# Small loads, turned conv tails, a split weight pair and token products reordered in a one-core decoder step

## The reference

```python
h = rmsnorm(x, norm_mix)
(m_q, m_k, m_v, m_i, m_f, m_o, g_qkv, g_a, g_b, g_out, x_q,
 gate_a, gate_b, gate_c) = split(h @ w_in)
h_a, C1, n1, m1 = mlstm_chunked(...)            # matrix memory, 4 heads of 128
conv_in = concatenate([conv0, g_qkv], axis=1)   # causal conv of width 4
conv1 = conv_in[:, S:]                          # the conv tails: an output
h_b, S1 = gated_delta_chunked(silu(conv(conv_in)), ...)
h_c = memory_attention(x_q, mem_k, mem_v)       # prompt: rmsnorm(mem, mem_norm) @ w_mem_kv; samples: caches
mixed = (sigmoid(gate_a) * (h_a @ w_br_mlstm) + sigmoid(gate_b) * (h_b @ w_br_gdn)
         + sigmoid(gate_c) * (h_c @ w_br_xattn))
x = x + mixed @ w_out
x = x + hier_moe(rmsnorm(x, norm_ffn), ...)     # top-1 of 4 groups, top-2 of 4 experts in it
y = rmsnorm(x, final_norm)
```

## Time and profile before

| | |
|---|---|
| median of 3 runs | 776.87 us (774.41 to 777.2) |
| profiled execution, its own time | 773.82 us |
| its span, first to last instruction | 771.7 us |
| PE busy | 716.7 us |
| DVE busy | 274.6 us |
| ACT busy | 164.5 us |
| bytes moved by DMA | 187.25 MB |
| mean granted TensorE clock | 0.98 |

### The profile page before, as it was taken

How to read it: one execution, slowest core, us unless ns; L and a number is a source line. 1 busy time by engine, 2 the same in 40 slices (tenths; PEclk the granted TensorE clock), 3 DMA queues, 4 the chain that set the end, 5 groups by cost and what they waited for, 6 DMA issues and landing times.

```text
span 771.7 us, 10609 instructions
## 1 busy us (share of the span) xinstructions
PE 716.7 (93%) x4393; PEld 422.0 (55%) x4393; DVE 274.6 (36%) x732; ACT 164.5 (21%) x377; POOL 62.3 (8%) x93
## 2 busy tenths in 40 slices
PE   6999999999989999999999999999999877878784
PEld 3544457877656777777777775543333323323331
DVE  1242013566763761464154352250232101100245
ACT  3221212222455411321131211231010000000014
POOL 3010200010330100000010020020000000001110
PEclk9999999999999999999999999999999989999998
DMA  9983700661399502023325487677999999999991
GB/s 271 343 284 109 192 27 1 236 252 72 96 393 371 187 6 106 1 84 138 109 73 214 138 278 315 243 314 259 391 424 427 407 429 430 411 425 398 431 358 64
DMA packets 49471, 187.25 MB, mean 243 GB/s; under 512 B 5240, under 2 KB 5485, under 8 KB 45322
## 3 DMA queue, kind: packets, MB, share of 16 engines
q1 hardware_dynamic: 40032, 155.52, 52.1%
q0 software_dynamic: 9280, 30.96, 12.1%
q10 hardware_dynamic: 106, 0.03, 0.0%
HBM read 174.43 MB, written 16.83 MB: 248 GB/s over the span
## 4 chain that ended last, share of the span: by engine, by line
PE 74%; DMA 15%; DVE 5%; ACT 2%; issue 2%; SPq 1%; POOL 1%; ACTq 0%; DVEq 0%
PE PS L664 13%; PE PS L1011 12%; DMA arena<-in_w_exp_down 9%; PE PS L1428 8%; PE PS L1023 6%; PE PS L1458 6%; PE PS L753 5%; DMA ring<-in_w_exp_down 3%; PE PS L675 2%; PE PS L780 2%; DMA out_C_s<-ring 2%; PE PS L650 2%; PE PS L1310 2%; PE PS L739 1%; SPq L1533 1%
## 5 line engine op out<-in xcount | busy, mean ns | idle before, releaser
L1428 PE MATMUL PS<-ring,arena 128*64 128x512 f32 x416 | 98.5, 629 | 13.7 <-issue 13.7
L1011 PE MATMUL PS<-hT,ring 128*128 128x288 f32 x384 | 102.2, 414 | 0.0
L1762 ACT ACTIVATE arena<-PS 128x512 f32<-128x512 f32 (+7 forms) x128 | 51.0, 422 | 183.5 <-PE PS L664 51.3
L1011 PEld LDWEIGHTS PS<-hT,ring 128*128 128x128 f32 x384 | 70.1, 190 | 19.6 <-issue 1.5
L1428 PEld LDWEIGHTS PS<-ring,arena 128*64 128x64 f32 x416 | 34.6, 144 | 73.0 <-issue 73.0
L664 PE MATMUL PS<-ring,hT 128*128 128x512 f32 x160 | 70.3, 596 | 0.0
L1762 ACT ACTIVATE brT<-PS 128x256 f32<-128x256 f32 (+4 forms) x37 | 15.6, 424 | 200.1 <-PE PS L1428 152.6
L1023 PE MATMUL PS<-brT,ring 128*128 128x288 f32 x192 | 50.5, 412 | 0.3 <-DVE arena L2557 0.3
L664 PEld LDWEIGHTS PS<-ring,hT 128*128 128x128 f32 x160 | 29.9, 190 | 37.3 <-issue 37.3
L753 PE MATMUL PS<-hT,ring 128*128 128x288 f32 x192 | 49.3, 410 | 0.9 <-DVE small L2325 0.9
L2968 DVE SCALAR_TENSOR_TENSOR brT<-brT,PS 128x256 f32<-128x256 f32 x16 | 6.7, 421 | 113.5 <-ACT brT L1762 113.5
(11 more groups left out here) (393 smaller groups left out, 866.9 us busy)
## 6 DMA issues: line engine op xcount, KB each, us to landing
ring<-in_w_in SPq DMA_DIRECT2D x15, 2048.0 KB, 10.3
ring<-in_w_exp_gate SPq DMA_DIRECT2D x13, 2048.0 KB, 23.9
ring<-in_w_exp_up SPq DMA_DIRECT2D x13, 2048.0 KB, 26.3
ring<-in_w_exp_down SPq DMA_DIRECT2D x8, 2048.0 KB, 26.0
arena<-in_w_exp_down SPq DMA_DIRECT2D x6, 2048.0 KB, 29.8
arena<-in_w_exp_gate SPq DMA_DIRECT2D x3, 2048.0 KB, 17.6
arena<-in_w_exp_up SPq DMA_DIRECT2D x3, 2048.0 KB, 22.4
moe_in<-in_table SPq DMA_DIRECT2D x2, 2048.0 KB, 23.8
```

Source lines behind the costliest of these rows:

```text
L1011: ins = pe.matmul(PS[:, b, 0:T], w[:, 512 * k + 128 * (c % 4):512 * k + 128 * (c % 4) + 128], hT[:, k, :], start=(k == 0), stop=(k == KD - 1))
L1428: ins = pe.matmul(o[64 * hf:64 * hf + 64, :], hg[:, k, 64 * e:64 * e + 64], w[:, :, 512 * k + 256 * hf:512 * k + 256 * hf + 256], start=(k ...
L1762: return act.activation(o, i, f, **kw)
```

## The change

- The memory norm gets a tile of its own (`memrow`), loaded first on ACT's queue, turned into bank 7 and copied by DVE ahead of the first memory tile; the other five vectors are turned after the second memory tile.
- On ACT, `keys_out(4)` stands ahead of `silu(0)`, whose tanh waits for the output of C_s.
- The twelve transposes of the conv tails go from the end of the attention to behind the router's last logits; ACT's copies go behind the three normalised rows, ACT issues the two output DMAs itself, and DVE waits for these before its first write of selected slots (`hg` shares the memory). Old waits for them are gone. The fillers go from 4 and 3 to 3 and 1.
- Pair 4 (the down matrices of experts 0 and 1 of group 0) is loaded as four DMAs of 1 MB: two when PE has read half of pair 0's matrices, two when it has read all.
- In the last group `to_tokens(0, 0)` and `to_samples(0)` stand ahead of the third gate/up instead of behind it, with other banks, and DVE's additions move accordingly.
- The four loads of S signal one semaphore instead of four.

```diff
@@ tensor
-        pe.wait_ge(sg("vrow_in"), 16 * 6)
-        o = use("vec", 6)
-        pe.transpose(o[:, 0:NV], vrow, ident[0:NV, 0:NV]).then_inc(full[6], 1)
+        pe.wait_ge(sg("mem_norm_in"), 16)
+        o = use("memvec", 7)
+        pe.transpose(o[:, 0:KD], memrow, ident[0:KD, 0:KD]).then_inc(full[7], 1)
         pe.wait_ge(sg("xin4"), 16)
         turn_rows(4, (2, 3))
+        pe.wait_ge(sg("vrow_in"), 16 * 5)
+        o = use("vec", 6)
+        pe.transpose(o[:, 0:NV - KD], vrow, ident[0:NV - KD, 0:NV - KD]).then_inc(full[6], 1)
...
         read_memory(1)
-        pe.wait_ge(sg("tailT"), 1)
-        for g in range(3):
-            b = (0, 5, 6)[g]
...
         logits(1).then_inc(full[1], 1)
-        keep_busy(4)
+        pe.wait_ge(sg("tailT"), 1)
+        for g in range(3):
+            b = (0, 5, 4)[g]
+            o = use(("tail", g), b)
+            for c in range(4):
+                ins = pe.transpose(o[0:HIST * (NB + 1), 128 * c:128 * c + 128], tailT[:, 4 * g + c, :], ident)
+            ins.then_inc(full[b], 1)
+        keep_busy(3)
...
-        keep_busy(3)
+        keep_busy(1)
...
             down(0, p, g)
+            to_tokens(0, 0, p)
+            to_samples(0, p)
             gate_up(2, p, g)
-            to_samples(0, p)
-            to_tokens(0, 0, p)
             to_tokens(0, 1, p)
...
+                if (g, e, k) == (0, 0, KD // 2 - 1) and isinstance(p, int):
+                    ins.then_inc(sg("half_read"), 1)
@@ sync
+            if first and q == NPAIR:
+                sp.wait_ge(sg("half_read"), 1)
+                for ex in range(2):
+                    ...
+                    sp.dma_start(dst[:, 0:2, :], src[:, 0:2, :]).then_inc(sg("d_first"), 16)
+                sp.wait_ge(*last_reader(0, p))
+                for ex in range(2):
+                    ...
+                    sp.dma_start(dst[:, 2:4, :], src[:, 2:4, :]).then_inc(ring_full[gslot("d", ex, 0)], 16)
+                return
@@ gpsimd
-        pool.wait_ge(*taken(("tail", 2)))
-        pool.dma_start(out["conv_p"][0, 0], tails[0:HIST, :]).then_inc(sg("tail_out"), 16)
-        pool.dma_start(out["conv_s"][0].rearrange("b s c -> (b s) c"), tails[HIST:, :]).then_inc(sg("tail_out"), 16)
@@ scalar
+        act.dma_start(memrow, a["mem_norm"][0].rearrange("(r c) -> r c", c=128)).then_inc(sg("mem_norm_in"), 16)
...
+        keys_out(4)
         silu(0)
-        keys_out(4)
...
-        act.wait_ge(sg("Cp_out"), 16)
-        for g in range(3):
-            copy_out(("tail", g), tails[:, 512 * g:512 * g + 512], bank_of(("tail", g))[0:HIST * (NB + 1), :])
...
+        for g in range(3):
+            copy_out(("tail", g), tails[:, 512 * g:512 * g + 512], bank_of(("tail", g))[0:HIST * (NB + 1), :])
+        act.wait_ge(*taken(("tail", 2)))
+        act.dma_start(out["conv_p"][0, 0], tails[0:HIST, :]).then_inc(sg("tail_out"), 16)
+        act.dma_start(out["conv_s"][0].rearrange("b s c -> (b s) c"), tails[HIST:, :]).then_inc(sg("tail_out"), 16)
         act.wait_ge(sg("lge"), 1)
@@ vector
             if g == 0:
+                if isinstance(p, int):
+                    dve.wait_ge(sg("tail_out"), 32)
                 slots_out(0, p, 0)
...
                     add_rows(0, p, step)
+                    add_tokens(0, 0, 0, p)
+                    add_tokens(0, 0, 1, p)
+                    add_samples(0, p)
                 if (e, g) == (2, G - 1):
-                    add_samples(0, p)
-                    for nn in range(2):
-                        for t in range(2):
-                            add_tokens(0, nn, t, p)
+                    add_tokens(0, 1, 0, p)
+                    add_tokens(0, 1, 1, p)
```

More of the change, by code:

```diff
@@ L160, in build @@
     tailT = tiny(128, NCT, HIST * (NB + 1))
-    V_MIX, V_MEM, V_ML, V_GD, V_FFN = 0, KD, 2 * KD, 2 * KD + H, 2 * KD + H + 1
+    V_MIX, V_ML, V_GD, V_FFN = 0, KD, KD + H, KD + H + 1
     V_N0 = V_FFN + KD
+    V_MEM = V_N0 + NB * H
     cwT = tiny(128, NCT, NB * HIST + CW)
@@ L250, in build @@
     wg, p = place(p, 128, KD, 16)
-    vrow, p = place(p, NV, 128)
+    vrow, p = place(p, NV - KD, 128)
+    memrow, p = place(p, KD, 128)
     crow, p = place(p, NB * HIST + CW, CCH)
@@ L290, in build @@
     qwm, _ = place(M0 + NB * DA, 128, H, NB, NS)
-    tails, _ = place(M0 + 4 * W, HIST * (NB + 1), CCH)
+    tails, _ = place(M0, HIST * (NB + 1), CCH)
     mixed, p = place(B0, 128, KD, T)
@@ L1188, in _ @@
                 hp = [slice(NS * h, NS * h + NS) for h in range(H)]
-                for h in range(H):
-                    pe.wait_ge(sg(f"Ss_in{h}"), 16)
+                pe.wait_ge(sg("Ss_in"), 16 * H)
                 pe.wait_ge(sg("qdm"), 1)
@@ L1451, in down @@
                         pe.wait_ge(*gready("d", 2 * pr_ + x, p, g))
+                    if (g, pr_) == (0, 0) and isinstance(p, int):
+                        pe.wait_ge(sg("d_first"), 32)
                 pe.wait_ge(*gtaken("dn", 2 * pr_ + nn, p, g))
@@ L1506, in load_pair @@
             s_ = PAIR_SLOTS[q % NPAIR]
+            if first and q == NPAIR:
+                sp.wait_ge(sg("half_read"), 1)
+                for ex in range(2):
+                    src = a["w_exp_down"][0, ex].rearrange("(c p) n -> p c n", p=128)
+                    dst = gunit("d", ex, 0).rearrange("p (c n) -> p c n", c=4)
+                    sp.dma_start(dst[:, 0:2, :], src[:, 0:2, :]).then_inc(sg("d_first"), 16)
+                sp.wait_ge(*last_reader(0, p))
+                for ex in range(2):
+                    src = a["w_exp_down"][0, ex].rearrange("(c p) n -> p c n", p=128)
+                    dst = gunit("d", ex, 0).rearrange("p (c n) -> p c n", c=4)
+                    sp.dma_start(dst[:, 2:4, :], src[:, 2:4, :]).then_inc(ring_full[gslot("d", ex, 0)], 16)
+                return
             if q >= NPAIR:
@@ L1762, in run @@
             return act.activation(o, i, f, **kw)
+        act.dma_start(memrow, a["mem_norm"][0].rearrange("(r c) -> r c", c=128)).then_inc(sg("mem_norm_in"), 16)
         r = 0
-        for x, n in ((a["norm_mix"][0], KD), (a["mem_norm"][0], KD), (a["mlstm_norm"][0], H),
-                     (a["gdn_norm"][0], 1), (a["norm_ffn"][0], KD)):
+        for x, n in ((a["norm_mix"][0], KD), (a["mlstm_norm"][0], H), (a["gdn_norm"][0], 1), (a["norm_ffn"][0], KD)):
             act.dma_start(vrow[r:r + n, :], x.rearrange("(r c) -> r c", c=128)).then_inc(sg("vrow_in"), 16)
@@ L2041, in _ @@
             part_at(t, "X0")
-            if t == 0:
-                act.wait_ge(sg("tail_out"), 32)
-            else:
+            if t:
                 act.wait_ge(*filled(("hbT", t - 1)))
@@ L2217, in mark @@
             dve.memset(scrap[:, marks[0]:marks[0] + 1], 0.0).then_inc(sem_, n)
-        dve.wait_ge(*filled("vec"))
-        cp(vecT, bank_of("vec")[:, 0:NV]).then_inc(freed("vec"), 1)
-        dve.wait_ge(*taken("vec"))
+        dve.wait_ge(*filled("memvec"))
+        cp(vecT[:, V_MEM:V_MEM + KD], bank_of("memvec")[:, 0:KD]).then_inc(freed("memvec"), 1)
+        dve.wait_ge(*taken("memvec"))
         for j in (3, 4, 0, 1, 2):
@@ L2224, in _ @@
             if j == 0:
+                dve.wait_ge(*filled("vec"))
+                cp(vecT[:, 0:NV - KD], bank_of("vec")[:, 0:NV - KD]).then_inc(freed("vec"), 1)
+                dve.wait_ge(*taken("vec"))
                 for i, (_, m) in enumerate(TILES):
```

5 lines of the change are left out of this document (2 added, 3 removed).

## The result

The changed kernel takes 770.57 us (median of 7 runs, 767.09 to 772.47) against 777.11 for the kernel before beside it (7 runs, 774.29 to 779.03): ratio 0.9927, 95% interval 0.9908 to 0.9945, so 4.3 to 7.1 us faster. A second series (experiment 8) gave 771.27 (11 runs) against 774.43 (16 runs), ratio 0.994, interval 0.9919 to 0.996: 3.1 to 6.3 us. The forecast was 770.9 and 6.0 us.

What follows compares the result with a forecast made beforehand. The prediction took a PE chain to bound the kernel until the weight stream fills at 539.81, then bytes. Its terms, 4.5 us ahead and 1.5 behind, make 6.0 off the median 776.87: 770.9 us, range 766.5 to 775.5.

Steps and rivals of the forecast that it cites:

- start of kvK: At the kernel's start, the norm's own load lets the first projection matmuls begin near 10.2 instead of 11.57: 1.4 us.
- keys' copy: In the key turns, copying keys before the tanh shortens PE's 1.86 us wait: 1.2 us, ends 0.6 and 1.6.
- tails out of the middle: After attention, the transposes only cover a wait (0), but ACT's lighter load removes a later PE wait: 0.4 us.
- ranks to first gate/up: In the routing, one filler instead of three after the ranks starts row picking earlier: 1.5 us, ends 1.2 and 1.7.
- Rival 4: In the routing, tail outputs land late and DVE's wait delays the first gate/up: slower, 787.2 us; chance 0.07.
- Halves: Loading the fifth pair in halves: its first halves go earlier, but the sixth pair does not: 0, ends 0 and 0.5.
- Rival 3: At the fifth pair, the halves pay in full by closing the stream's gap before 541: 3.4 us more, 767.5; chance 0.05.
- A fallen clock in the routing is no rival: In the routing, the new PE gaps of 0.2 and 1.7 us would not lower the clock: no cost.
- Token products: In the last group, products before the third gate/up start the fourth near 738.8, not 740.31: 1.5 us, ends 0 and 3.1.
- The stream ends as much earlier as it begins: For the weight stream, the gain at its start, 4.5 us, is passed on to its end; otherwise the prediction fails.
- Fails if the sixth pair is not earlier by 3 us: Failure sign at the sixth pair's issue: expected near 535.3 instead of 539.81, and failing if less than 3 us earlier.
- rival 2: At the start, the clock rises earlier during the first projection: up to 2.6 us more, 768.3; chance 0.15.

Runs made afterwards that it cites:

- experiment 8: The changed kernel taken again unaltered, for a second profile, against the kernel before: 771.27 us, ratio 0.994.
- after: First profile of the changed kernel, the slowest of its seven runs: 772.47 us, span 770.6; the series' median is 770.57 us.
- after again: Second profile of the unaltered changed kernel, from experiment 8, the fastest execution of its series: 768.23 us, span 766.4.
- p_front: Kernel before with only the memory norm's own load added: 773.78 us, ratio 0.9986.
- n_swap: Changed kernel with ACT's sample softmax and output gate's copy and tanh moved ahead of the second memory read's copy: 767.15 us, ratio 0.9897 to the kernel before.
- n_warm: Changed kernel with ten unread matmuls before the first memory tile and three before the first kvK matmul: 769.21 us, ratio 0.9916 to the kernel before.
- n_both: Changed kernel with n_swap's order on ACT and n_warm's unread matmuls together: 766.52 us, ratio 0.9879 to the kernel before.
- p_tails: Kernel before with only the conv tails moved to the routing, fillers at 3 and 3: 775.28 us, ratio 0.9992.
- p_fillers: Kernel before with only the fillers behind the ranks cut from three to one: 775.20 us, ratio 0.9988.
- p_halves: Kernel before with only the fifth pair loaded in halves: 775.28 us, ratio 0.9999.
- p_keys: Kernel before with only the keys' copy put ahead of the tanh: 774.78 us, ratio 0.9993.
- p_tokens: Kernel before with only the token and sample products put ahead of the last group's third gate/up: 774.37 us, ratio 0.9993.
- p_delay: Kernel before with eleven fillers instead of three behind the ranks, a known delay: 781.15 us, ratio 1.0075.

## Why the prediction was right, and where it was off

The terms, as won against the profile of before, in us:

| term | forecast | after | after again | alone |
|---|---|---|---|---|
| start of kvK | 1.4 | 1.27 | 1.39 | 1.48 |
| clock during kvK | 0 | 0.16 | 2.45 | 2.45 |
| keys' copy | 1.2 | 1.07 | 1.24 | 0.84 |
| tails out of the middle | 0.4 | 0.58 | 0.58 | 0.59 |
| ranks to first gate/up | 1.5 | 1.33 | -0.05 (with a dip) | 1.41 |
| dips elsewhere | 0 | -3.38 | 0 | |
| **sixth pair** | **4.5** | **1.02** | **5.60** | |
| behind it, to the last output's issue | 1.5 | 1.05 | 0.64 | 1.0 |
| last issue to the end of the span | 0 | -0.97 | -0.94 | |
| **span** | **6.0** | **1.1** | **5.3** | |

The rows add up within 0.02. Point by point:

- *Norm, keys, tails, fillers:* mechanisms right. With dips and early clock taken out they give 4.2 us in the first profile, and 4.5 in the second if the filler term is put at the first's 1.33, for 4.5 forecast. The keys' copy was put at 1.2 with ACT as what comes next; alone it was 0.84, because the load of the keys came next as well (0.41), in the changed kernel 1.07 and 1.24.
- *Fillers ahead of the ranks and the wait for the tails' outputs:* no cost, as forecast. Rival 4 had no start: DVE waited for PE, 11 us after the issue.
- *Halves:* 0 as forecast. Rival 3 falls.
- *"A fallen clock in the routing is no rival":* wrong as argued. Its rows were two groups that took 7.09 with and without idle before them, but in the same trace five of the expert groups between 600 and 700 us took 8.63 to 9.53, and the picks ran longer by 1.67 with their filler in two of six profiles with one filler (experiment 8). There the filler term is worth nothing.
- *Token products:* the interval shrank by 1.57 as forecast, but the step "the second half of the down product finds the stream ended" failed: it waits 0.46 alone and 1.03 in the second profile. The term is 0.6 to 1.1, not 1.5. The slack between the last bytes and their reader was smaller than what was taken from it.
- *The stream ends as much earlier as it begins:* right. Adding the DMA shares of the last slices of 1 us to the start of the first of them, it ends at 750.95 before, 749.90 after and 745.30 after again: 1.05 and 5.65 earlier, for 1.02 and 5.60.
- *"Fails if the sixth pair is not earlier by 3 us":* in the profiled execution it was not (1.02), and the reason is neither edit nor order but 3.4 us of dips; in the second it was 5.60. The test was put on one trace, and one trace carries up to two dips of 1.7.
- *The clock:* the assumption that the rise moves with the matmuls holds in one of four profiles with the norm's own load. In the other three (`p_front`, `n_swap`, after again; not after) the 32 records took 14.00 us, in the seven without it 15.48 to 17.07. That is rival 2 in traces, but each of the three is the fastest execution of its series and after's is the slowest, and the median of `p_front` moved by 1.07. So among timed executions the early rise is probably the smaller part. In both profiles with the unread matmuls (`n_warm`, `n_both`) the 32 records took 14.00: what PE does before 10 us bears on it. The Trainium skill ("TensorE: Matmul & The Clock Gate", section on the clock gate) has sustained activity release the full rate. These five early starts agree; after's late one, with the same matmuls as after again's, shows that the order alone does not settle it.
- *The end:* not in the prediction at all, see below.

So the mechanisms were mostly right, and that the median hit 770.9 within 0.4 us is partly luck. First, the 6.0 were taken from a median of 3 runs, 776.87, and the kernel before took 774.43 to 774.95 in the three later series: 2 us less. From there 6.0 leads to 768.4 to 769.0, and the changed kernel's 770.57 and 771.27 are 3.2 to 4.4 us below these medians, not 6. Second, without dips and without the early clock both profiles come to the same sum: 4.2 to 4.5 ahead of the stream, 1.05 and 0.64 behind it, and 0.95 given back at the end, of which about 0.2 comes back because the time exceeds the span by 2.1 us before and by 1.8 to 1.9 after. That is an estimate of 4.5 to 4.6 us of time for both; the two ratios give 5.7 and 4.6. The 6.0 lie within both intervals but above all of these, and the terms that were too large are the token products (0.6 to 1.1 instead of 1.5) and the end, which was put at nothing. Seven of thirteen profiles have a dip ahead of the stream (after, `p_tails`, `p_fillers`, `p_halves`, `n_both`, after again, `n_warm`). The parts alone have ratios whose product is 0.995, against 0.9927 and 0.994 together; with intervals of 0.2% each that is no contradiction, and only the milestones in the traces tell the parts apart.

## What to carry to other kernels

Find the point from which the DMA stream is full, and read every edit by how far it moves the instruction that starts the stream: ahead of it a microsecond of PE chain is a microsecond of the end, whether won or lost. Work that covers a wait is free where it stands, but taking it away uncovers the wait: repairing that (here an order on ACT, 1.95 us) was worth more in the traces than any one part of the change without the early clock. A forecast time is a base plus a change: take the base from many runs, or the change may look right when it isn't. Judge parts of a microsecond by intervals between milestones of a trace, not by one span, and compare the length of identical groups first to see where the clock dipped.

## What was not expected of the hardware

- **The clock dips while PE is fully busy.** In 494 to 496 us of the changed kernel's first profile PE is busy 2.00 of 2 us, as it is in all of 420 to 494, and the granted clock is 0.50. Between the transposes near 260 us and the ranks such a dip shows in two of thirteen profiles (after, `p_tails`: 249.05 and 249.07 us instead of 247.36). Dips of the same cost, 1.7 us, stand behind a short idle of PE: in the conv fill (0.86 us idle before it, 5.81 instead of 4.12) in five (after, `p_tails`, `p_fillers`, `p_halves`, `n_both`), in the picks in two. What sets their place stays open. The expert groups of 8.4 to 10.1 us instead of 7.09 between 590 and 730 us are another matter: every profile has some, the kernel before too, in the stretch where the DMA is full and PE waits (2.80 us before the one at 705.56).
- **The end is 0.95 us longer in some kernels.** From the issue of the last output to the end of the span it is 4.0 to 4.1 us before and in `p_keys`, `p_fillers`, `p_halves`, `p_tokens` and `p_delay`, and 4.9 to 5.0 in both profiles of after, `p_front`, `p_tails`, `n_swap`, `n_warm` and `n_both`. In before and after the last DMA's traffic is over some 3 us after the issue, and what follows has no busy engine. Two parts bring it each by itself, the norm's own load and the moved tails, and both together bring it once. The number of DMAs on ACT's queue does not explain it: `p_front` issues six there, as the kernel before does. Its cause stays open.
